# Two hybrid transformer blocks in one kernel: work of the first and the third mixer in another order

## What is computed

```python
# first mixer: latent attention (8 heads) and grouped attention (8 heads), each with its own gate
z = rmsnorm(x, g_mix) @ w_in
q_lat, kv_lat, qb, kb, vb, gate_a, gate_b = split(z)
qa  = rmsnorm(q_lat) @ w_qb            # 8 heads, 64 + 32 rotated columns
kva = rmsnorm(c_kv) @ w_kvb            # keys and values; k_pe (32 rotated columns) is shared by the heads
merged = sigmoid(gate_a) * (oa @ w_oa) + sigmoid(gate_b) * (ob @ w_ob)
x = x + merged @ w_o

# third mixer ("odd"): sparse attention with a token selection
q, ckv, q_idx, k_idx, w_idx = split(h @ w_in)
score = sum_h w_idx[h] * relu(q_idx[h] @ k_idx)      # 8 index heads, causal
idx   = top_k(score, 64)                             # 64 keys of each query
s = q_lat @ c[idx] + bias[distance]                  # 16 heads
x = x + (softmax(s) @ c[idx] @ w_uv) @ w_out
```

## Time and profile before

| what | us |
|---|---|
| median of 3 executions | 1370.14 (1369.77 to 1370.59) |
| the profiled execution | 1369.89 |
| its span, first to last instruction | 1367.9 |
| PE busy | 1343.2 (98%) |
| DVE busy | 973.5 (71%) |
| ACT busy | 676.8 (49%) |
| POOL busy | 70.1 (5%) |
| mean granted clock of TensorE | 0.995 |

### The profile page before, as it was taken

How to read it: one execution, slowest core, us unless ns; L and a number is a source line. 1 busy time by engine, 2 the same in 40 slices (tenths; PEclk the granted TensorE clock), 3 DMA queues, 4 the chain that set the end, 5 groups by cost and what they waited for, 6 DMA issues and landing times.

```text
span 1367.9 us, 19408 instructions
## 1 busy us (share of the span) xinstructions
PE 1343.2 (98%) x7680; PEld 1151.7 (84%) x7680; DVE 973.5 (71%) x1327; ACT 676.8 (49%) x1056; POOL 70.1 (5%) x109
## 2 busy tenths in 40 slices
PE   9999999999999999999999999999999999999998
PEld 6888988888888888898888888888888786888886
DVE  5786777666687777657667776776766698576675
ACT  6576454344554444456555444544444557444442
POOL 0300010000000000004000000000000034000000
PEclk9999999999999999999999999999999999999999
DMA  8433556655546655464446655566554463466551
GB/s 333 138 126 123 173 167 226 198 191 184 185 132 218 203 187 185 156 203 130 156 136 213 195 191 196 161 203 194 198 196 144 148 174 112 146 203 213 186 185 46
DMA packets 67594, 241.31 MB, mean 176 GB/s; under 512 B 7999, under 2 KB 8392, under 8 KB 67504
## 3 DMA queue, kind: packets, MB, share of 16 engines
q1 hardware_dynamic: 65200, 234.19, 51.9%
q0 software_dynamic: 2016, 5.77, 1.7%
q10 hardware_dynamic: 288, 0.11, 0.0%
HBM read 238.88 MB, written 1.09 MB: 175 GB/s over the span
## 4 chain that ended last, share of the span: by engine, by line
PE 86%; DVE 9%; ACT 2%; issue 2%; DMA 1%; POOL 0%; DVEq 0%; POOLq 0%; SPq 0%; ACTq 0%
PE pp L467 84%; DVE wlo L1703 3%; PE pp L476 2%; DVE fa L1703 1%; DVE pbuf L1707 1%; DVE hx L1711 1%; DVE xn L1912 1%; ACT whi L1258 1%; DVE fa L1803 0%; DMA raw<-w_chunks 0%; ACT hx L1259 0%; DVE fa L2285 0%; ACT pbuf L1409 0%; DMA fa<-f_rows 0%; DVE st L2281 0%
## 5 line engine op out<-in xcount | busy, mean ns | idle before, releaser
L1703 DVE TENSOR_TENSOR wlo<-raw,whi 128x1024 fp32r<-128x1024 f32 (+1 forms) x444 | 522.8, 1220 | 144.2 <-ACT whi L1258 143.8
L467 PE MATMUL pp<-hx,whi 128*128 128x512 f32 (+1 forms) x2400 | 543.7, 361 | 2.9 <-DVE fa L1803 1.1
L1258 ACT ACTIVATE whi<-raw 128x1024 fp32r<-128x1024 f32 (+1 forms) x444 | 441.6, 1043 | 94.8 <-PE pp L467 85.9
L467 PEld LDWEIGHTS pp<-hx,whi 128*128 128x128 f32 x2400 | 421.6, 189 | 75.1 <-issue 9.3
L467 PE MATMUL pp<-whi,ra 128*128 128x512 f32 x1144 | 366.1, 391 | 0.0
L467 PE MATMUL pp<-hx,wlo 128*128 128x256 f32 x2032 | 315.4, 279 | 0.0
L467 PEld LDWEIGHTS pp<-hx,wlo 128*128 128x128 f32 x2032 | 279.6, 188 | 9.9
L467 PEld LDWEIGHTS pp<-whi,ra 128*128 128x128 f32 x1144 | 214.6, 188 | 43.7 <-issue 0.9
L467 PE MATMUL pp<-wlo,ra 128*128 128x512 f32 x572 | 222.8, 389 | 0.0
L1803 DVE TENSOR_REDUCE fa<-pp 128x512 f32<-128x1024 f32 x104 | 127.0, 1221 | 73.2 <-PE pp L467 73.1
L1258 ACT ACTIVATE ra<-fa 128x512 fp32r<-128x512 f32 x63 | 39.8, 632 | 228.1 <-DVE fa L1711 228.1
(11 more groups left out here) (175 smaller groups left out, 778.0 us busy)
## 6 DMA issues: line engine op xcount, KB each, us to landing
raw<-w_chunks SPq DMA_DIRECT2D x438, 512.0 KB, 5.2
fa<-t_rows POOLq DMA_DIRECT2D x16, 128.0 KB, 3.7
fx<-x_t SPq DMA_DIRECT2D x2, 512.0 KB, 6.4
X<-x_in SPq DMA_DIRECT2D x2, 512.0 KB, 7.6
fa<-g_fin POOLq DMA_DIRECT2D x2, 512.0 KB, 4.2
fa<-f_rows POOLq DMA_DIRECT2D x8, 128.0 KB, 3.3
raw<-w_chunks SPq DMA_DIRECT2D x3, 256.0 KB, 6.0
cst<-consts POOLq DMA_DIRECT2D x1, 576.0 KB, 7.5
```

The costliest lines, as they stand in the source:

```text
L467: return pe.matmul(o, lhs, rhs, start=first, stop=last, skip_group_check=True)
L1258: return act.activation(o, i, ACT.Copy, scale=1.0)
L1703: return dve.tensor_tensor(o, a, b, op)
```

## The change

In the first mixer gate 2 goes ahead of the key's transposes, the key's copy moves from DVE to ACT, DVE's splits after `gate1` move behind the rotation of the queries, and the entry to attention waits for one copy instead of three. The output product uses bank 7 first and waits for the gates' banks one by one. In the third mixer half of `qi1` is computed ahead of a wait, each head's `ckv` part stands ahead of its index product, `q0` goes to bank 6, the selection rounds start ahead of DVE's splits, one split is done in a pair of heads (pairs 0 to 7), the numbers of steps change, and bank 3 serves for one head more.

```diff
         STEPS = {"first": {0: (9, 0, 0)}, "fox": {0: (12, 0, 0), 4: (6, 3, 3)},
-                 "odd": {0: (6, 0, 0), 2: (3, 1, 0), 3: (2, 1, 2), 4: (2, 1, 2), 6: (2, 1, 1), 7: (2, 1, 1), 8: (2, 1, 1)}}
+                 "odd": {0: (7, 0, 0), 2: (3, 1, 0), 5: (3, 0, 0), 6: (2, 1, 1), 7: (2, 1, 1), 8: (2, 1, 1)}}
...
-            return 3 if h % 2 and h < (4 if name == "fox" else 12) else 6
+            return 3 if h % 2 and h < (4 if name == "fox" else 14) else 6
...
+                    elif name == "first" and b == 3:
+                        pe.wait_ge(s_qbe, 3)
...
-            def out_half(nm, c, n, banks):
+            def out_half(nm, c, n, banks, gates=0):
...
+                    if gates and f % 2 == 0:
+                        pe.wait_ge(s_gmul, gates - 1 + f // 2)
...
-                pe.wait_ge(s_kpe, 6)
-                pe.wait_ge(s_ka, 1)
-                for t in range(2):
-                    y = tp(ps[0][0:96, 128 * t:128 * t + 128], kp[:, t, :])
-                y.then_inc(s_kpT)
                 pe.wait_ge(s_ka, 3)
                 for _ in gate(2, 2):
                     pass
+                pe.wait_ge(s_kpe, 6)
+                pe.wait_ge(s_ka, 1)
+                for t in range(2):
+                    y = tp(ps[0][0:96, 128 * t:128 * t + 128], kp[:, t, :])
+                y.then_inc(s_kpT)
                 pe.wait_ge(s_qkr, 4)
...
-                    pe.wait_ge(s_gmul, 8)
-                    yield from out_half("oa", 0, 0, (2, 7))
+                    yield from out_half("oa", 0, 0, (7, 2), 8)
...
-                        pe.wait_ge(s_qbe, 3)
+                        pe.wait_ge(s_qbe, 1)
...
+                weights_ready(IDX["qi1"])
+                b_part("qi1", 6, range(4), True, False)
                 pe.wait_ge(s_hl, 8 * 7 + 8)
                 kw_part(range(4, 8)).then_inc(s_done)
...
-                gemm_b("qi1", hh, hl, range(8), 256, two_halves(6)).then_inc(s_done)
+                b_part("qi1", 6, range(4, 8), False, True).then_inc(s_done)
...
-                pe.wait_ge(s_ki, 16)
-                pe.wait_ge(s_qit, 2)
+                pe.wait_ge(s_qit, 1)
                 for h in range(8):
+                    for t in range(2):
+                        a = slice(256 * h, 256 * h + 256)
+                        y = mm3(ps[4 + t][:, 0:256], hh[:, h, tk(t)], hl[:, h, tk(t)], whi[:, i % NHL, a], wlo[:, i % NHL, a],
+                                h == 0, h == 7)
...
+                    if h == 1:
+                        pe.wait_ge(s_ki, 16)
+                    if h == 4:
+                        pe.wait_ge(s_qit, 2)
...
                 weights_ready(IDX["q0"])
+                pe.wait_ge(s_qit, 2)
+                gemm_b("q0", hh, hl, range(8), 256, two_halves(6)).then_inc(s_done)
                 pe.wait_ge(s_trow, 1)
-                gemm_b("q0", hh, hl, range(8), 256, two_halves(7)).then_inc(s_done)
...
-                            pe.wait_ge(s_ptc, HEAD0["odd"] + 12)
+                            pe.wait_ge(s_ptc, HEAD0["odd"] + 14)
...
-                    if causal and p < pairs:
+                    if name == "fox" and p < pairs:
                         one_more(p, 0)
                     one_more(p, 1)
...
-                tanh_gate(2)
+                act.wait_ge(s_kpT, 1)
+                copy(kaT[64:96, :, :], ps[0][64:96, 0:256].unsqueeze(1).to_broadcast([32, 8, 256])).then_inc(s_kpc)
                 for j in range(4):
                     act.wait_ge(s_qaT, j + 1)
                     copy(qaT[0:96, 2 * j:2 * j + 2, :], two(ps[4 + j][0:96, :])).then_inc(s_qae)
+                tanh_gate(2)
                 after("wqb")
...
-                after("ckv")
                 act.wait_ge(s_ck, 2)
...
                 y.then_inc(s_cksq)
+                after("ckv")
                 after("q0")
...
                 after("uk")
+                split_at["odd", -1, 1] = next_half[0]
```

On DVE, in the first mixer and in the third (`top_round` is shortened to the places that move):

```diff
-                after("gate1")
                 for t in range(2):
                     for c in range(2):
...
                     tt(qv, t1, t2, ALU.add).then_inc(s_qkr)
+                after("gate1")
                 gate_mul(2)
-                dve.wait_ge(s_kpT, 1)
-                copy(kaT[64:96, :, :], ps[0][64:96, 0:256].unsqueeze(1).to_broadcast([32, 8, 256])).then_inc(s_kpc)
...
-                merge(0, (2, 7), (0, 1))
+                merge(0, (7, 2), (0, 1))
...
-                after("ckv")
...
-                dve.wait_ge(s_cksq, 1)
-                ts(st[:, 2:4], st[:, 0:2], 1.0 / 256, EPS, ALU.mult, ALU.add).then_inc(s_ckm)
...
                 top_round(0)
+                dve.wait_ge(s_cksq, 1)
+                ts(st[:, 2:4], st[:, 0:2], 1.0 / 256, EPS, ALU.mult, ALU.add).then_inc(s_ckm)
+                top_round(1)
                 dve.wait_ge(s_ckr, 1)
...
-                top_round(1)
-                turned_("q0", qT, 0, 7, s_qT)
+                after("ckv")
+                top_round(2)
+                turned_("q0", qT, 0, 6, s_qT)
                 half_split()
...
-                after("uk")
+                half_split()
```

More of the change, by code:

```diff
@@ L864, in first_mixer @@
                 y.then_inc(s_done)
+                pe.wait_ge(s_ka, 3)
+                for _ in gate(2, 2):
+                    pass
                 pe.wait_ge(s_kpe, 6)
@@ L869, in first_mixer @@
                 y.then_inc(s_kpT)
-                pe.wait_ge(s_ka, 3)
-                for _ in gate(2, 2):
-                    pass
                 pe.wait_ge(s_qkr, 4)
@@ L1138, in odd_mixer @@
                 b_part("qi0", 5, range(4, 8), False, True).then_inc(s_done)
-                weights_ready(IDX["qi1"])
-                gemm_b("qi1", hh, hl, range(8), 256, two_halves(6)).then_inc(s_done)
+                b_part("qi1", 6, range(4, 8), False, True).then_inc(s_done)
                 pe.wait_ge(s_kw, 1)
@@ L1146, in odd_mixer @@
                 weights_ready(i)
-                pe.wait_ge(s_ki, 16)
-                pe.wait_ge(s_qit, 2)
+                pe.wait_ge(s_qit, 1)
                 for h in range(8):
+                    for t in range(2):
+                        a = slice(256 * h, 256 * h + 256)
+                        y = mm3(ps[4 + t][:, 0:256], hh[:, h, tk(t)], hl[:, h, tk(t)], whi[:, i % NHL, a], wlo[:, i % NHL, a],
+                                h == 0, h == 7)
+                    if h == 7:
+                        y.then_inc(s_done)
                     b = h % 4
@@ L1158, in odd_mixer @@
                     y.then_inc(s_ix)
-                    for t in range(2):
-                        a = slice(256 * h, 256 * h + 256)
-                        y = mm3(ps[4 + t][:, 0:256], hh[:, h, tk(t)], hl[:, h, tk(t)], whi[:, i % NHL, a], wlo[:, i % NHL, a],
-                                h == 0, h == 7)
-                y.then_inc(s_done)
                 pe.wait_ge(s_wi, 1)
@@ L1171, in odd_mixer @@
                     for t in range(2):
-                        y = tp(ps[6][:, 256 * k + 128 * t:256 * k + 128 * t + 128], xn[:, t, k * 128:(k + 1) * 128])
+                        y = tp(ps[7][:, 256 * k + 128 * t:256 * k + 128 * t + 128], xn[:, t, k * 128:(k + 1) * 128])
                 y.then_inc(s_ckvT)
@@ L1663, in odd_mixer @@
                 for k in range(2):
-                    copy(ch[:, k, :], ps[6][:, 256 * k:256 * k + 256], scale=G("g_ckv")[:, k:k + 1]).then_inc(s_ch)
+                    copy(ch[:, k, :], ps[7][:, 256 * k:256 * k + 256], scale=G("g_ckv")[:, k:k + 1]).then_inc(s_ch)
                 after("q1")
@@ L1929, in attention @@
                         evict((name, p, 0))
-                    if causal:
+                    if name == "fox":
                         lows(p - 1, 0)
@@ L2300, in odd_mixer @@
                     ts(xn[:, t, 0:256], ck[:, t, :], st[:, 4 + t:5 + t], None, ALU.mult, None).then_inc(s_yc)
-                top_round(1)
-                turned_("q0", qT, 0, 7, s_qT)
+                after("ckv")
+                top_round(2)
+                turned_("q0", qT, 0, 6, s_qT)
                 half_split()
-                top_round(2)
-                half_split()
+                top_round(3)
                 dve.wait_ge(s_ch, 2)
                 for k in range(2):
-                    stt_(cl[:, k, :], ps[6][:, 256 * k:256 * k + 256], G("g_ckv")[:, k:k + 1], ch[:, k, :].bitcast(F),
+                    stt_(cl[:, k, :], ps[7][:, 256 * k:256 * k + 256], G("g_ckv")[:, k:k + 1], ch[:, k, :].bitcast(F),
                          ALU.mult, ALU.subtract).then_inc(s_cl)
-                top_round(3)
+                half_split()
+                top_round(4)
                 turned_("q1", qT, 1, 4, s_qT)
                 half_split()
-                top_round(4)
+                top_round(5)
                 half_split()
-                for r in range(5, 8):
+                for r in range(6, 8):
                     top_round(r)
```

## The result

| what | before | after |
|---|---|---|
| median of 4 executions, us | 1370.08 (1369.77 to 1370.59) | 1357.17 (1356.69 to 1358.49) |
| the profiled execution | 1369.89 | 1357.3 |
| its span | 1367.9 | 1355.3 |
| mean granted clock | 0.995 | 0.998 |

What follows compares the result with a forecast made beforehand. PE was taken as the bound, busy 1343.2 of 1367.9 us, with DVE ending many of its waits. From 1369.9, 3.3 for the first mixer and 7.1 for the third gave 1359.5 us, range 1356.7 to 1364.2.

Steps and rivals of the forecast that it cites:

- First mixer, 3.3: First mixer: scores of head 0 start 2.5 us earlier and the output product's wait goes, 0.8; together 3.3.
- Third mixer up to the scores, 5.5: DVE reaches first scores 5.5 us earlier: last index sum 1.0, selection's wait 2.85, next split's wait 0.47, moved split 1.15.
- The third wait: Third mixer: PE's wait of 0.77 us ahead of q0 goes; no term, since PE is ahead of DVE.
- the fall at 1091: Third mixer, behind q0: lower-clock stretch expected to go, 1.6 us for PE, but no term of its own.
- the pay-back: Third mixer's pairs: the split moved behind the scores is done by pair 5, so the 5.5 lead becomes 4.9 us.
- 2.4 for q3's scaling: Third mixer, pair 5: DVE scales q3 before the reciprocals, so pair 6's scores start 2.4 us earlier still.
- a sign against the forecast: Third mixer, pairs 0 to 4: forecast wrong if PE waits more than 2 us in all for ACT's copies.
- rival 1: Third mixer: the pairs give DVE's lead back, yielding only 3 to 5 us; 1362 to 1364, chance 0.18.
- Rival 2: First mixer: the run of transposes lowers the clock, so 3.3 becomes 1.6; 1361.2 us, chance 0.08.
- Rival 3: Waits in pairs 2 to 4 and the new 1.0 in the first mixer vanish too; 1356.5 us, chance 0.08.
- Rival 4: Both mixers: waits only change their names, ACT being late or binding every pair; 1367.5 to 1370 us, chance 0.04.
- Rival 5: Third mixer: a clock fall follows each of eight pairs, costing 13.6 us; slower at 1373.1, chance 0.02.

Runs made afterwards that it cites:

- e_copy_dve: Changed kernel with the key's 32x2048 copy back on DVE, behind the multiply of gate 2; median 1360.35 us.
- e_gate2_behind: Changed kernel with gate 2 behind the key's two transposes again; median 1357.91 us.
- e_splits_ahead: Changed kernel with DVE's two splits ahead of the selection again, ACT's order staying as changed; median 1363.09 us.
- e_q0_wait: Changed kernel with q0 waiting for the copy of the bias row again, its bank staying 6; one execution, 1358.74 us.
- e_two_splits: Changed kernel with two splits a pair of heads in the third mixer again; median 1360.04 us.
- e_long_transposes: Changed kernel with the key's two transposes done 40 times over, 78 more transposes in one run; one execution, 1366.93 us.
- both halves: Two runs on the kernel before: the first mixer's edits alone, median 1366.77 us, and the third mixer's edits alone, median 1362.86 us.
- e_old_steps: Changed kernel with the old numbers of steps in the third mixer's fills, q3 ending in pair 5's last fill; median 1361.60 us.
- The repetition: The changed kernel run again with nothing altered; median 1358.74 us, ratio 0.9923 to the kernel before.
- e_first: Kernel before with only the first mixer's part of the change; median 1366.77 us, ratio 0.9978.
- e_norm_act: Changed kernel with the scaling of the third mixer's normed keys moved from DVE to ACT; median 1357.69 us, ratio 0.9903 to before.

## Why the prediction came out as it did

**First mixer, 3.3, measured 3.84.** Every step held in kind: no wait ahead of the key's transposes, a new one ahead of gate 3, the copy on ACT, no wait at the output product (1.01, not 0.8). The sizes were a little off. The wait ahead of gate 3 is 0.70 and not 1.0, but PE also came to it later than said, so that gate 3 starts only 0.13 earlier than forecast (67.65 + 1.02 = 68.67, where the text has 68.8). The text had the scores start when ACT was ready, at 73.6. They start at 73.34 on the same count (72.32 + 1.02), with no wait behind PE's own transposes: ACT's list was shorter than said, its first copy of the B queries starts at 71.58 + 1.02 = 72.60 and takes 0.6. That both moves carry part of the gain is shown by taking them back, in e_copy_dve (1.74) and e_gate2_behind (0.74).

**Third mixer up to the scores, 5.5, measured 5.23.** Of the four terms, 1.0 + 2.85 + 0.47 + 1.15, the last three stand. The first was 0.8, since the wait for `X` had grown by 0.26. e_splits_ahead shows that DVE's order there is worth even more (4.5) once PE's waits and the clock are drawn in. The third wait was rightly given no term: e_q0_wait has it again and ends at the same time. That the fall at 1091 was rightly given none is not shown, since no run has this fall with the rest of the changed order.

**The pairs.** The step that failed is the pay-back: "Up to pair 5 both orders do the same splits, six, so the one moved is paid back: 5.5 - 1.15 + 0.5 = 4.9 at pair 5". Measured was 5.46. From the first maxima to those of pair 5 DVE does four splits before and five after, so the moved one is there, but the stretch takes 24.05 before and 23.82 after. The intervals between the maxima show where. Behind pair 0's, one split more adds only 0.11 (4.15 before, 4.26 after). It stands in place of the wait of 0.50 and adds 0.56 with that, as forecast, but the two scalings of the weights behind it take 0.43 less (from start to start 0.68 + 1.39 before, 0.97 + 0.67 after), which the step did not foresee; they run beside POOL (last section). Behind pair 1's and pair 2's together, one split in each instead of two in pair 1 saves 0.38 (5.76 + 4.65 before, 4.25 + 5.78 after). e_two_splits puts a price of 1.36 on heaping in the new order. The next step, 2.4 for q3's scaling, was measured as 7.80 - 5.46 = 2.34. The waits for ACT's copies in the pairs make 2.44 together, over the 2 that I had named as a sign against the forecast. The sign was badly chosen: before, two such waits made 2.25 already. The other sign holds, DVE has no idle row ahead of its reciprocals, so rival 1 did not come about.

**The other rivals.** Rival 2 (transposes lower the clock) is refuted by e_long_transposes. Rival 3 named a number close to the median, 1356.5, but its cause did not occur: the waits of 0.70 and of about 1 in the pairs are still there. Rival 4 is refuted by both halves. Rival 5 (a fall in each pair) did not occur; e_old_steps shows that one fall can come there, and 2.0 us were lost with it.

**Sum.** 1369.9 - 3.84 - 7.80 = 1358.3 is what the steps would have given with their measured sizes. The profiled 1357.3 lies another 1.0 lower by the start, which was luck. The median of 1357.17 lies as low; its other executions have no profile, so how much of that is the start is not known. The repetition's median is 1358.74. So of the 2.2 by which the forecast of 1359.5 lies above the profiled execution, 0.5 belong to the first mixer, 0.7 to the third and about 1 to the start.

## What to carry to other kernels

Where an engine's list paces a stretch, look for the entry that waits and put work behind it that waits for nothing: a wait of 2.85 is the largest term of the 7.8 here, putting it back cost 4.5, and 0.55 more taken off the list came out as 0.54 and 0.58. Spread optional work evenly over the rounds of such a stretch, and place a result that another engine needs directly ahead of its need; where a wait grew from 0.8 to 2.0 it cost 3.5 here, with a fall of the clock behind it. Compare traces between fixed instructions, not by medians, when terms are under 1 us and the start wanders by 3.2.

## What the runs showed of the hardware that was not expected

**The start.** The first mark lies between 42.55 and 45.72 in 14 profiles, though the kernels issue the same instructions up to there. It goes in the main with PE's wait for the first low part: 1.15 us in e_first, 1.61 after, 1.89 before, 2.94 in e_splits_ahead (e_norm_act, at 44.18 with 1.66, is an exception). In the five profiles with 1.15 to 1.66 the clock stays at 1.00 around 8 to 12 us; in the nine with 1.89 to 2.94 it falls to 0.50 (for 3.4 us, before; for 6.8 in e_splits_ahead). Windows, after and e_splits_ahead:

```profile
8.00:12.00 4.00, 3.51 (x14) 2.63 (x15) 3.43 (x7) 3.69 (x6) 0.00 (x0) 1.00 1.03 396
```

```profile
8.00:15.00 7.00, 6.28 (x15) 4.98 (x16) 6.71 (x11) 6.68 (x12) 0.21 (x1) 0.52 1.01 389
```

**DVE's scaling beside POOL.** Two scalings of the weights take 0.55 on DVE when POOL is idle and up to 1.75 beside POOL's sums. The splits too take 1.6 instead of 1.21 when POOL's sums run into them. After, DVE at the end of pair 2 and in pair 6, and POOL:

```profile
1120.56 1.75 DVE L1719 TENSOR_SCALAR pbuf<-pbuf,st 128x128 f32<-128x128 f32 x2
...
1138.84 0.55 DVE L1719 TENSOR_SCALAR pbuf<-pbuf,st 128x128 f32<-128x128 f32 x2
```

```profile
1120.99 1.16 POOL L2478 TENSOR_TENSOR fa<-fa 128x128 f32<-128x128 f32 x2
```

POOL's sums end at 1122.15 and DVE's scaling at 1122.3. POOL has nothing to do between 1137.7 and 1141, where the short one lies. This agrees with the Trainium skill (SBUF — State Buffer, Terms), by which the two engines share a pair of ports that one holds for its whole instruction while the other stands. I did not try it by moving POOL's sums, so the cause is argued and not shown. At most 1.2 us lie in this one place (1.75 less 0.55), an estimate, in a stretch that DVE paces.
